# Recurrent mixer of a hybrid trunk: the passes of the head-pair loop interleaved, with another order inside the scan

## The reference

```
def step(S, inp):                                  # one token, one head
    w_t, k_t, v_t, kk_t, a_t = inp[:5]
    S = (S * w_t[:, :, None, :]
         - jnp.einsum('bhvk,bhk->bhv', S, kk_t)[..., None] * (kk_t * a_t)[:, :, None, :]
         + v_t[..., None] * k_t[:, :, None, :])
    return S, (jnp.einsum('bhvk,bhk->bhv', S, inp[5]) if emit else None)
...
for d in range(2):                                 # forwards and backwards
    S_c, o_c = rwkv7_scan(*seq(ctx), S0, emit=need_ctx_out)
    _, o_l = rwkv7_scan(*seq(lat), S_c, emit=True)
    o_lat = o_lat + rev(o_l)
...
mu = jnp.mean(o, axis=-1, keepdims=True)           # readout: group norm, bonus, gate
var = jnp.mean(jnp.square(o - mu), axis=-1, keepdims=True)
y = ((o - mu) * lax.rsqrt(var + GN_EPS) * gn_w + gn_b)
bonus = sum(jnp.sum(s['r'] * kd * rw['r_k'], axis=-1, keepdims=True) for kd in s['k']) * s['v']
y = y + bonus
g = jax.nn.sigmoid(s['glo']) @ rw['g_up']
return y * g
```

## Time and profile before

| | |
|---|---|
| median of 3 runs | 3763.72 us (3758.34 to 3766.32) |
| the profiled execution: its time, and its span | 3755.34 us, 3753.7 us |
| TensorE busy | 3343.5 us, 89% |
| VectorE busy, ScalarE busy | 1902.8 us, 1381.7 us |
| mixer stage, first product to last output | 835.2 to 1740.5 us of the span |
| one pass of it | 113.3 us |

### The profile page before, as it was taken

One profiled execution on the slowest core, in us unless ns is written; L12 is line 12 of the kernel. 1 busy time (PEld: TensorE's weight loads), 2 busy tenths in 40 slices (PEclk: granted clock), 3 DMA queues, 4 the chain that ended last, 5 costly groups with the idle time before them and its releaser, 6 DMA issues.

```text
span 3753.7 us, 49721 instructions
## 1 busy us (share of the span) xinstructions
PE 3343.5 (89%) x19488; PEld 2722.8 (73%) x19488; DVE 1902.8 (51%) x2220; ACT 1381.7 (37%) x1591; POOL 91.0 (2%) x148
## 2 busy tenths in 40 slices
PE   6799996659888898887899999997998979999999
PEld 1588885337665667665688888886987768888887
DVE  0522321664554444553545555555698555555554
ACT  1322211444543444443333434343445333333332
POOL 1000000110000000000000000000000000000000
PEclk8799998769888999898999999998999989999999
DMA  9634432774345544346666565656650465556563
GB/s 358 214 124 130 157 104 86 258 240 159 108 161 188 179 145 144 112 166 227 189 191 191 179 192 190 191 191 179 191 180 1 148 180 200 182 191 189 192 190 135
DMA packets 320145, 650.16 MB, mean 173 GB/s; under 512 B 15499, under 2 KB 20321, under 8 KB 316641
## 3 DMA queue, kind: packets, MB, share of 16 engines
q1 hardware_dynamic: 300000, 597.04, 47.6%
q0 software_dynamic: 8896, 35.95, 3.9%
q10 hardware_dynamic: 11104, 15.01, 1.1%
HBM read 634.22 MB, written 13.60 MB: 173 GB/s over the span
## 4 chain that ended last, share of the span: by engine, by line
PE 79%; DVE 9%; DMA 7%; ACT 3%; issue 2%; ACTq 1%; POOL 0%; SPq 0%; DVEq 0%; POOLq 0%
PE ps L397 41%; PE ps L415 12%; PE ps L417 6%; PE ps L944 6%; DMA raw<-in_ada_w_dram 4%; PE ps L955 3%; PE ps L338 2%; PE ps L1400 2%; DMA gate<-mod_scratch 2%; DVE rw_scl L784 1%; PE ps L1782 1%; PE ps L919 1%; DVE rw_t L756 1%; DMA at_qk<-qkv_scratch 1%; PE ps L979 1%
## 5 line engine op out<-in xcount | busy, mean ns | idle before, releaser
L374 DVE TENSOR_TENSOR split_lo<-raw,split_hi 128x2048 fp32r<-128x2048 f32 (+1 forms) x372 | 850.2, 2288 | 1079.7 <-ACT split_hi L364 1034.0
L364 ACT ACTIVATE split_hi<-raw 128x2048 fp32r<-128x2048 f32 (+1 forms) x372 | 710.3, 1911 | 1309.3 <-PE ps L397 974.5
L415 PE MATMUL ps<-xa,split_hi 128*128 128x512 f32 x2048 | 720.2, 397 | 19.8 <-DVE split_lo L374 11.6
L417 PE MATMUL ps<-xa,split_lo 128*128 128x256 f32 x2048 | 574.7, 281 | 0.0
L415 PEld LDWEIGHTS ps<-xa,split_hi 128*128 128x128 f32 x2048 | 386.4, 189 | 113.2 <-issue 23.3
L397 PE MATMUL ps<-split_hi,hT_lo 128*128 128x512 f32 x1024 | 398.9, 390 | 0.0
L397 PE MATMUL ps<-split_hi,hT_hi 128*128 128x512 f32 x1024 | 398.9, 390 | 0.0
L397 PE MATMUL ps<-split_lo,hT_hi 128*128 128x512 f32 x1024 | 398.9, 390 | 0.0
L417 PEld LDWEIGHTS ps<-xa,split_lo 128*128 128x128 f32 x2048 | 389.3, 190 | 0.0
L338 PE MATMUL ps<-raw,s 128*32 128x512 f32 x1536 | 219.6, 674 | 45.5 <-DMA raw<-in_ada_w_dram 45.4
L397 PEld LDWEIGHTS ps<-split_hi,hT_hi 128*128 128x128 f32 x1024 | 192.3, 188 | 40.2
(11 more groups left out here) (327 smaller groups left out, 4619.1 us busy)
## 6 DMA issues: line engine op xcount, KB each, us to landing
raw<-in_mlp_w_dram SPq DMA_DIRECT2D x256, 1024.0 KB, 5.6
raw<-in_ada_w_dram SPq DMA_DIRECT2D x192, 1024.0 KB, 8.5
raw<-in_mix_in_w_dram SPq DMA_DIRECT2D x48, 1024.0 KB, 5.2
raw<-in_conv_pw_w_dram SPq DMA_DIRECT2D x48, 1024.0 KB, 5.5
gate<-mod_scratch POOLq DMA_DIRECT2D x16, 1024.0 KB, 8.3
raw<-in_mix_out_w_dram SPq DMA_DIRECT2D x16, 1024.0 KB, 6.0
qkv_scratch<-hbuf ACTq DMA_DIRECT2D x20, 256.0 KB, 3.8
rwkv_scratch<-hbuf ACTq DMA_DIRECT2D x18, 256.0 KB, 2.2
```

What stands on the lines that cost most here:

```text
L364: nc.scalar.activation(split_hi[:, c, :, 0:n], raw[:, c, :, 0:n], ACT.Copy).then_inc(hi_done, 1)
L374: nc.vector.tensor_tensor(split_lo[:, c, :, 0:n], raw[:, c, :, 0:n], split_hi[:, c, :, 0:n], ALU.subtract).then_inc(lo_done, 1)
L415: pe.matmul(ps[:, base + j, :], split_hi[:, c, kk, j * P:(j + 1) * P], both, start=(k == 0), stop=False, skip_group_check=True)
L417: mm = pe.matmul(ps[:, base + j, 0:SEQ], split_lo[:, c, kk, j * P:(j + 1) * P], xa_hi[:, k, :], start=False, stop=(k == KT - 1), skip_grou ...
```

## The change

The mixer's code is cut into functions of a pass `x` (class `Pass`: a loop register and an offset), and each engine calls those of the next pass and of the last pass inside the current one. The loops now run over passes 1 to 6; pass 0 and pass 7 are written out ahead and behind.

- The next pass's preparation stands in this pass's scan: on TensorE and ScalarE wholly, on VectorE from the decayed keys on. VectorE's token shifts for it stand in this pass's inverse (steps 15 to 25). It has two PSUM banks of its own, 5 and 7, in turn (`PREP`).
- The readout of a pass stands in the next pass's scores and inverse, in bank 5 (`EPI`): mean and centring ahead of and in the scores, variance in them, gate product behind step 5, VectorE's steps at 6 to 11. The bonus stands in its own pass's inverse (steps 12, 13, 16, 21).
- The four modulation pieces of the preparation stand in the inverse (steps 8, 12, 18, 22). All pieces use one accumulator (bank 4) where there were two.
- In the scan the state update stands ahead of the outputs, the state has two buffers, and the outputs go part by part over the four instances and not instance by instance.
- VectorE masks the last chunk's scores behind the first two steps of the inverse.
- The scores go through six banks in another order, and the transposes too.

Cut to what matters, first the banks:

```diff
-        SCB = [2, 3, 6, 7, 0, 1]
+        SCB = [7, 2, 6, 0, 1, 3, 7, 2, 6, 0, 7, 1, 2, 3, 1, 2]
+        TRB = [3, 6, 0, 1, 3]
+        EPI = 5
+        PREP = [5, 7, 5, 7, 5, 7, 5, 7, 5]
```

The loads by GpSimd's queue, each of which runs one pass further ahead:

```diff
+            load_inputs(Pass(0, 0))
+            with pool.Fori(0, HEADS - 1) as i:
+                load_inputs(Pass(i, 1))
+                load_gate_up(Pass(i, 0))
+            load_gate_up(Pass(0, HEADS - 1))
```

ScalarE's scan and pass:

```diff
                 for c in range(4):
-                    act.wait_ge(W["rh_ps"], i * 4 + (c + 1))
+                    act.wait_ge(W["rh_ps"], x.n(4, c + 1))
...
-                    if c:
-                        act_ada(act, *rwkv_ada(i, c), i * ADA_R + (Q_RW + c), 1 - c % 2, i * 32 + ((0, ST_T)[c % 2] + 16 * (c // 2)))
+                    if c == 0:
+                        ada_rows(x, 0)
+                        if not last:
+                            rates(x.next())
+                    elif c == 1:
+                        if not last:
+                            decays(x.next())
+                        ada_rows(x, 1)
+                        if not last:
+                            key_norm(x.next())
+                    elif c == 2:
+                        if not last:
+                            exponentials(x.next(), (0, 1))
+                    else:
+                        ada_rows(x, 2)
+                        if not last:
+                            exponentials(x.next(), (2, 3))
+                if not last:
+                    turned(x.next())
+                ada_rows(x, 3)
+
+            def body(x, first, last):
+                if not first:
+                    deviation(x.last())
+                inverse(x)
+                scan(x, last)
```

VectorE's scan and pass:

```diff
+                    if c == 2 and not last:
+                        key_scale(x.next(), 0)
+                    dve.wait_ge(W["st_ps"], x.n(3, c + 1))
...
+                    if c == 0 and not last:
+                        decayed_keys(x.next())
                     if c == 2:
-                        dve.wait_ge(W["o_ps"], i * 2 + 1)
+                        if not last:
+                            key_scale(x.next(), 1)
+                        dve.wait_ge(W["o_ps"], x.n(2, 1))
...
+            def body(x, first, last):
+                inverse(x, first, last)
+                scan(x, last)
+                if not last:
+                    unit_keys(x.next())
+                    scaled_keys(x.next(), 0)
+                    scaled_keys(x.next(), 1)
+                outputs(x)
+                if not last:
+                    scaled_queries(x.next())
```

TensorE's inverse, and the outputs:

```diff
+                    if k == 5 and not first:
+                        gates(x.last())
+                    elif k == 16:
+                        bonus(x)
+                    elif k in (8, 12, 18, 22):
+                        ada_chunk(x, (8, 12, 18, 22).index(k))
...
+            def outputs_of(c):
+
+                for part in range(3):
                     for inst in range(4):
...
+                        mm = pe.matmul(o, l, r, start=(part == 0 and d == 0), stop=(part == 2), skip_group_check=True)
+                mm.then_inc(W["o_ps"], 1)
```

More of the change, by code:

```diff
@@ L133, with __init__, n, ds @@
 SCAN = [[0, 1, 2, 3], [1, 0, 3, 2]]
-RW_DVE = 31
+RW_DVE = 36
+class Pass:
+    def __init__(self, reg, off):
+        self.reg, self.off = reg, off
+    def n(self, per, c=0):
+        return self.reg * per + (self.off * per + c)
+    def ds(self, n, first=0):
+        return bass.ds(self.reg * n + (self.off * n + first), n)
+    def next(self):
+        return Pass(self.reg, self.off + 1)
+    def last(self):
+        return Pass(self.reg, self.off - 1)
 def rwkv_memory(nc):
@@ L615, in rwkv_act @@
             W = rws
+            four = lambda b: ps[:, b, :].rearrange("p (t s) -> p t s", t=4)
             for j, r0 in enumerate((WL0, AL0)):
@@ new lines, in bonus, with inverse @@
+            def bonus(x):
+                pe.wait_ge(W["pr"], x.n(1, 1))
+                pe.wait_ge(W["y"], x.n(1, 1))
+                pe.matmul(ps[:, EPI, SEQ:TOK], R["blk"][:, :], R["t12"][:, 1, 0:SEQ], start=True, stop=True).then_inc(W["bon_ps"], 1)
+            def inverse(x, first):
+                for c in range(4):
+                    if c == 0 and not first:
+                        mean(x.last())
+                    scores(x, c, first)
+                    if c == 2 and not first:
+                        variance(x.last())
@@ new lines, in scan, with body @@
+                if not last:
+                    turn(x.next(), 0)
+                ada_chunk(x, 14)
+                ada_chunk(x, 15)
+                if not last:
+                    for n in range(1, 5):
+                        turn(x.next(), n)
+            def body(x, first, last):
+                inverse(x, first)
+                scan(x, last)
+            p0, p7 = Pass(0, 0), Pass(0, HEADS - 1)
+            rates(p0, lambda: None)
+            decays(p0, 0)
+            decays(p0, 1)
```

681 lines of the change are left out of this document (441 added, 240 removed).

## The result

The changed kernel takes 3668.1 us (median of 4 runs, 3666.8 to 3680.9) against 3763.4 for the kernel before: a ratio of 0.9756, 95% interval 0.9732 to 0.9780. It is faster by 95 us, where 163 were forecast (3600), and lies outside the range of 3574 to 3640. The profiled execution has a span of 3665.1 us, 88.6 less than before's 3753.7.

The account below looks back on a forecast made before the run. TensorE bounds inverse and scan, VectorE's maskings the scores, no engine the readout and preparation. A pass: 79.6 + 13.8 - 3.2 = 90.2 us, 23.1 less; seven times, 162 off 3763.7 gives 3602, rounded to 3600; range 3574 to 3640.

Parts of the forecast that it names:

- A stretch of the pass under a clock of 0.9: Sign to look for in a pass: no stretch would have a granted clock below 0.9.
- The third sign: Pieces waiting for transfers, listed after low clock in the scan and TensorE idle over 8 us as proving the prediction wrong.
- slower: Rival: the preparation is strung into the scan without overlap, a pass takes 117.2 us, 3795 in all; chance 0.03.
- transfers: Rival: modulation pieces wait for their transfers in the scan, up to 2 us per pass, 3616; 0.22 together with the chain.
- inverse with pieces, gate, bonus: Inverse, 40.1 us before, takes in four pieces (4.0 us), gate products (1.15) and bonus (0.6): expected at 45 us.
- scan with preparation: Scan, 30.6 us before, takes in the next pass's products, rates and transposes at full clock: expected at 35 to 37 us.
- scores; mean and variance: Scores stay at 8.9 us; mean and variance there count 0, since TensorE waits anyway, with 1.2 us as upper bound.
- a piece: One modulation piece on TensorE: 1.0 us from start to start, the group expected to stay at that.
- outputs of a chunk: 24 instructions in the scan fall from 2.9 us to 2.0 by alternating array halves, 1.8 us less per pass.
- preparation and readout, 23.1 less per pass: The fourth stretch, 33.7 us, no longer stands between passes; with the work moved elsewhere, 23.1 us less, seven times: 162.
- at the ends: Eighth pass's pieces and gate product (+2.5) against a cheaper first preparation (-2 to -3): 0.
- The table loads: ScalarE: 1.28 us each, nothing behind them, four per pass; rival with a 1.38 us drain each gives 3612, chance 0.03.

Follow-up runs that it names:

- a_shift50: The changed kernel with 50 more instructions on TensorE (waits already met) ahead of the mixer's loop, nothing else changed: 3607.8 us, 0.9570 of before.
- a_shift150: The changed kernel with 150 more instructions on TensorE (waits already met) ahead of the mixer's loop, nothing else changed: 3661.7 us, 0.9729 of before.

## Why the prediction was wrong, point by point

**The branch was priced at nothing.** The sum took instructions, waits and clock, and no step of it asked what a loop's end costs. In before it costs nothing twice over: the loop's code stays, and a wait of 3.77 us would hide most of a fetch. The change puts one pass ahead of the loop, which moves it to 8 blocks, and takes the wait away. At a_shift50's position the kernel takes 3607.8 us, inside the range and 8 from the forecast; 60.3 of the 68 us of error are the position. By the spans it is 48.5 in the mixer and 11.9 behind it, less 4.6 ahead of it. That 3607.8 comes so near is in part luck: of the 162 us that were to leave the mixer 149.3 do, and by the spans a_shift50 saves 144.4 (3753.7 - 3609.3). The sum took its 162 off the median, and before's profiled execution lay 8.4 under the median, a_shift50's not.

**The criteria were the right ones.** "The prediction is wrong if TensorE's idle time in a pass exceeds 8 us": it is 10.2 us in the pass shown (101.35 - 91.10). A stretch of the pass under a clock of 0.9 was a sign too, and the first row of the pass has 0.63. The third sign, pieces that wait for transfers, came as well but small: 6.3 us in 950 to 1550. No rival had the branch: "slower" strung the preparation into the scan, and "transfers" held pieces up, and neither happened at this size.

**The pass itself**, forecast against a_shift50's rows (and the changed kernel's, where they differ):

| term | forecast | measured |
|---|---|---|
| inverse with pieces, gate, bonus | 45.0 | 45.40 |
| scan with preparation | 36.3 | 35.95 (37.24) |
| scores; mean and variance | 8.9; 0 | 9.12 (10.29); 0.53 |
| a piece | 1.0 | 1.0 |
| outputs of a chunk | 2.0, bounds 1.45 and 2.9 | 1.76; 3.23 in the old order |
| pass | 90.2 | 91.0 (101.35) |
| preparation and readout, 23.1 less per pass | 162 in all | 149.3 in the mixer |

The products of the preparation did run at the full clock, the VectorE steps did fit the inverse, and the decays (L1163) start with no wait for the sigmoids. 7 x 22.4 = 157 come from the passes by the means' mean spacing (90.8, the last one without a preparation). The other difference is at the ends, which I had put at 0: from first rates to first mean a_shift50 takes 113.3 us and before 105.6, since the first pass bears its own preparation alone (2.4 less than before up to its inverse) and the next one's in its scan, with the pieces (10 more). That is +7.7, the one term of the sum besides the branch that was mis-sized by more than 5 us.

**The table loads** came as forecast. ScalarE at the first one in a scan of the changed kernel:

```profile
1113.79 0.72 ACT L678 ACTIVATE rw_t<-rw_k,rw_cur 128x512 f32<-128x512 f32 x1 [0.83 <-ACT line L377]
1114.53 1.28 ACT L681 ACT_TABLE_LOAD   x1
1115.83 1.27 ACT L681 ACTIVATE rw_a<-ps,rw_cur 128x512 f32<-128x512 f32 x2
```

0.02 us lie on either side of the 1.28, so the drain of about 1.38 us that the Trainium skill names for it (page "ScalarE: Activation LUTs", section "What ACT_TABLE_LOAD costs") shows here neither ahead nor behind.

**What stays open.** The changed kernel has a second gap, 1.9 to 2.7 us ahead of the first score, that a_shift150 hasn't, with as many packets; which block each one waits for wasn't traced. The first rates start between 835 and 859 us in these kernels, mostly later with more instructions ahead; why wasn't tried.

## What to carry to other kernels

When a loop is peeled or grows, count where its code begins and ends, look for packets on the instruction queue inside it, and look for idle time "issue" at its first product; if they are there, move the loop or shorten it before judging the change. The version to keep here is a_shift50, 4.3% faster than before, and its fifty idle instructions are a stopgap for an aligned loop. Where a loop can't be kept whole, hold large transfers back until its branch is past.

A wait that is removed may have covered, or been about to cover, something that no profile of the kernel before shows. Ask of each long idle stretch what else happens during it.

## What the runs showed of the hardware

- A loop of TensorE over 7 blocks of 16 KB ran without a fetch; over 8 blocks all of it was loaded again in each pass (8 to 9 packets), though it is only 6.6 blocks long. The count of blocks rests on an offset of 18 to 35 instructions, which is inferred.
- A fetch at the branch held TensorE for 1.7 to 2.4 us with the modulation's loads small or held back, and for 4.5 to 4.7 with loads of 387 GB/s under way (a_shift150 and the changed kernel).
- Products of 64 columns that write alternate halves of the array took 0.073 us per instruction (24 in 1.76 us), six in a row on one half and one place 0.135 (24 in 3.23).
- With the same work, 0 to 150 instructions of padding moved the time between 3607.8 and 3668.1 us, 1.7%, more than the readout's overlap (51) or the outputs' order (26) is worth.
